# Byte displacements of the TensorE operands inside their SBUF buffers, by place in the turn, stage and chunk

## What is computed

```python
h = x + 0.5 * swiglu(rmsnorm(x), w1g, w1u, w1d)           # FFN 1
B, C, V, Z, Gc, Gp = split(rmsnorm(h) @ w_in)             # one input projection
y_conv = (B * conv3(C * V)) @ w_conv_out                  # 3 taps, causal
y_pool = grouped(trailing means of Z) @ w_pool_group      # windows 2, 4, 8, 16
h = h + (sigmoid(Gc) * y_conv + sigmoid(Gp) * y_pool) @ w_o
h = h + 0.5 * swiglu(rmsnorm(h), w2g, w2u, w2d)           # FFN 2
y = rmsnorm(h)
```

## Time and profile before

| | |
|---|---|
| median of three runs | 2799.03 us |
| the profiled execution, its own time | 2799.0 us |
| its span, first to last instruction | 2797.2 us |
| TensorE, matmuls busy | 2780.8 us, 99% of the span |
| VectorE busy | 1537.5 us, 55% |
| ScalarE busy | 1052.3 us, 38% |
| DMA | 412.27 MB, 147 GB/s |

### The profile page before, as it was taken

The page is one execution under the profiler, slowest core; times in us unless marked ns, Lnnn a source line. Parts: engine busy times, 40 slices in busy tenths (PEclk is TensorE's granted clock), DMA queues, the critical chain, the costliest instruction groups (busy, mean ns, idle before and its releaser), DMA issues.

```text
span 2797.2 us, 47809 instructions
## 1 busy us (share of the span) xinstructions
PE 2780.8 (99%) x18725; PEld 2777.2 (99%) x18725; DVE 1537.5 (55%) x2166; ACT 1052.3 (38%) x1283; POOL 12.3 (0%) x22
## 2 busy tenths in 40 slices
PE   8999999999999999999999999999999999999998
PEld 8999999999999999999999999999999999999998
DVE  6555455554555585555555555575555555555555
ACT  5333333333333453333333334363333333333334
POOL 0000000000000000000000000000000000000000
PEclk9999999999999999999999999999999999999999
DMA  6444444444444444444445444454444444444443
GB/s 196 151 143 142 139 146 142 142 142 142 142 143 143 141 137 151 151 149 141 157 138 158 151 150 142 150 158 151 151 150 150 150 150 150 150 150 150 150 150 105
DMA packets 347876, 412.27 MB, mean 147 GB/s; under 512 B 13039, under 2 KB 283503, under 8 KB 347446
## 3 DMA queue, kind: packets, MB, share of 16 engines
q1 hardware_dynamic: 347264, 410.24, 46.4%
q0 software_dynamic: 560, 1.32, 0.2%
HBM read 408.42 MB, written 3.32 MB: 147 GB/s over the span
## 4 chain that ended last, share of the span: by engine, by line
PE 98%; ACT 1%; DVE 0%; issue 0%; DMA 0%; SPq 0%; ACTq 0%; DVEq 0%
PE bank L408 33%; PE bank L409 33%; PE bank L407 32%; DMA acc<-in_x_sample 0%; ACT tb L710 0%; ACT w_hi L670 0%; PE bank L654 0%; SPq L312 0%; DVE w_lo L925 0%; DVE tok L997 0%; DVE xn_lo L978 0%; ACT h L729 0%; DVE h L1094 0%; PE bank L628 0%; PE bank L474 0%
## 5 line engine op out<-in xcount | busy, mean ns | idle before, releaser
L925 DVE TENSOR_TENSOR w_lo<-raw,w_hi 128x1024 fp32r<-128x1024 f32 x772 | 944.0, 1226 | 1037.7 <-ACT w_hi L670 1036.7
L670 ACT ACTIVATE w_hi<-raw 128x1024 fp32r<-128x1024 f32 x772 | 815.0, 1058 | 1341.6 <-PE bank L409 1340.4
L407 PE MATMUL bank<-xn_hi,w_hi 128*128 128x320 f32 (+2 forms) x4224 | 1314.1, 311 | 2.7 <-DVE xn_lo L978 2.7
L409 PE MATMUL bank<-xn_hi,w_lo 128*128 128x320 f32 (+2 forms) x4224 | 1316.3, 312 | 0.0
L408 PE MATMUL bank<-xn_lo,w_hi 128*128 128x320 f32 (+2 forms) x4224 | 1312.0, 311 | 0.0
L407 PEld LDWEIGHTS bank<-xn_hi,w_hi 128*128 128x128 f32 x4224 | 793.6, 188 | 3.1 <-issue 3.1
L408 PEld LDWEIGHTS bank<-xn_lo,w_hi 128*128 128x128 f32 x4224 | 793.7, 188 | 0.0
L409 PEld LDWEIGHTS bank<-xn_hi,w_lo 128*128 128x128 f32 x4224 | 792.7, 188 | 0.0
L408 PE MATMUL bank<-hid_lo,w_hi 128*128 128x320 f32 (+1 forms) x1952 | 608.2, 312 | 0.0
L409 PE MATMUL bank<-hid_hi,w_lo 128*128 128x320 f32 (+1 forms) x1952 | 606.5, 311 | 0.0
L407 PE MATMUL bank<-hid_hi,w_hi 128*128 128x320 f32 (+1 forms) x1952 | 600.0, 307 | 0.3 <-issue 0.3
(11 more groups left out here) (109 smaller groups left out, 489.1 us busy)
## 6 DMA issues: line engine op xcount, KB each, us to landing
raw<-in_w_ffn_gate SPq DMA_DIRECT2D x176, 512.0 KB, 3.5
raw<-in_w_ffn_up SPq DMA_DIRECT2D x176, 512.0 KB, 3.5
raw<-in_w_ffn_down SPq DMA_DIRECT2D x176, 512.0 KB, 3.6
raw<-in_w_in SPq DMA_DIRECT2D x176, 512.0 KB, 3.5
raw<-in_w_conv_out SPq DMA_DIRECT2D x32, 512.0 KB, 3.8
raw<-in_w_o SPq DMA_DIRECT2D x32, 512.0 KB, 3.7
raw<-in_w_pool_group SPq DMA_DIRECT2D x4, 512.0 KB, 4.0
out<-acc SPq DMA_DIRECT2D x8, 256.0 KB, 3.0
```

The lines of the kernel that those rows point to most:

```text
L407: pe.matmul(out, slot_hi(slot, col, col + P), hi, start=start, stop=False)
L409: return pe.matmul(out, slot_lo(slot, col, col + P), hi, start=False, stop=stop)
L670: act.activation(slot_hi(n % SLOTS), raw[:, n % RAW, :], ACT.Copy).then_inc(hi_done, 1)
L925: dve.tensor_tensor(slot_lo(n % SLOTS), raw[:, n % RAW, :], slot_hi(n % SLOTS).bitcast(F32), ALU.subtract).then_inc(lo_done, 1)
```

## The change

Nothing is added to or taken from the instructions. Only the places of operands inside their buffers change, and a slot becomes 64 floats (256 bytes) longer. Displacements are in floats of four bytes.

```diff
-XH_SHIFT, XL_SHIFT = (0, 0, 0, 0), (16, 8, 32, 48)
-HH_SHIFT, HL_SHIFT = (0, 0, 0, 0), (16, 16, 8, 8)
+XH_SHIFT = ((0, 0, 16, 16), (16, 16, 32, 32), (48, 48, 0, 0))
+XL_SHIFT = ((16, 8, 32, 48), (32, 24, 48, 40), (64, 56, 16, 8))
+HH_SHIFT = ((0, 0, 0, 0), (0, 0, 0, 0), (0, 0, 0, 0), (16, 16, 8, 8), (0, 0, 0, 0))
+HL_SHIFT = ((32, 32, 40, 40), (16, 16, 8, 8), (4, 4, 12, 12), (0, 0, 0, 0), (24, 24, 32, 32))
...
-SLOT = CHUNK
-WH_SHIFT, WL_SHIFT = (0, 0, 0, 0), (0, 0, 0, 0)
+SLOT = CHUNK + 64
...
+W_SPREAD = ((0, 0), (0, 8), (0, 0), (0, 8), (0, 16), (0, 16), (0, 32), (0, 32))
+W_FFN1 = 4 * ((0, 0),) + 4 * ((0, 8),) + 4 * ((0, 16),) + 4 * ((0, 32),) + W_SPREAD
+W_POOL = POOL_CHUNKS * ((0, 0),)
+W_CONV = (4 * ((0, 8),) + 4 * ((0, 16),) + 4 * ((0, 32),) + 4 * ((0, 0),) + 4 * ((0, 24),) + 4 * ((0, 4),)
+          + W_SPREAD)
+W_MIX = 4 * ((0, 8),) + 4 * ((0, 16),) + 4 * ((0, 32),) + 4 * ((0, 0),) + W_SPREAD
+W_FFN2 = 4 * ((0, 8),) + 4 * ((0, 16),) + 4 * ((0, 32),) + 4 * ((0, 24),) + W_SPREAD
+
+def w_place(n):
...
-        def x_hi(k, first):
-            at = k * ROW + XH_SHIFT[k // 4]
-            return xn_hi[:, at + first:at + T]
+        def x_hi(norm, k):
+            at = k * ROW + XH_SHIFT[norm][k // 4]
+            return xn_hi[:, at + first_of(norm):at + T]
...
-        def slot_lo(slot, first=0, last=CHUNK):
-            at = slot * SLOT + WL_SHIFT[slot]
+        def slot_lo(n, first=0, last=CHUNK):
+            at = n % SLOTS * SLOT + w_place(n)[1]
             return w_lo[:, at + first:at + last]
```

More of the change, by code:

```diff
@@ L78, with stage_of @@
 N_ALL = N_FFN2 + FFN_TURNS * FFN_CHUNKS
+W_SPREAD = ((0, 0), (0, 8), (0, 0), (0, 8), (0, 16), (0, 16), (0, 32), (0, 32))
[6 more added lines that the diff above has]
+def w_place(n):
+    if n < N_POOL:
+        return W_FFN1[(n - N_FFN1) % FFN_CHUNKS]
+    if n < N_CONV:
+        return W_POOL[n - N_POOL]
+    if n < N_MIX:
+        return W_CONV[(n - N_CONV) % CONV_CHUNKS]
+    if n < N_FFN2:
+        return W_MIX[(n - N_MIX) % MIX_CHUNKS]
+    return W_FFN2[(n - N_FFN2) % FFN_CHUNKS]
+def stage_of(n):
+    return sum(n >= first for first in (N_POOL, N_CONV, N_MIX, N_FFN2))
 B0, C0, V0, Z0, GC0, GP0 = 0, D, 2 * D, 3 * D, 3 * D + D // 2, 4 * D + D // 2
@@ L195, in build, with x_lo, g_hi, g_lo @@
         bank = [ctx.enter_context(nc.psum_tensor(f"bank{b}", [P, 512], F32)) for b in range(8)]
-        def x_hi(k, first):
-            at = k * ROW + XH_SHIFT[k // 4]
-            return xn_hi[:, at + first:at + T]
[L202 to L207, removed]
+        def x_hi(norm, k):
+            at = k * ROW + XH_SHIFT[norm][k // 4]
+            return xn_hi[:, at + first_of(norm):at + T]
+        def x_lo(norm, k):
+            at = k * ROW + XL_SHIFT[norm][k // 4]
+            return xn_lo[:, at + first_of(norm):at + T]
+        def g_hi(stage, t, width):
+            at = t * ROW + HH_SHIFT[stage][t]
             return hid_hi[:, at:at + width]
-        def g_lo(t, width):
-            at = t * ROW + HL_SHIFT[t]
+        def g_lo(stage, t, width):
+            at = t * ROW + HL_SHIFT[stage][t]
             return hid_lo[:, at:at + width]
-        def slot_hi(slot, first=0, last=CHUNK):
-            at = slot * SLOT + WH_SHIFT[slot]
+        def slot_hi(n, first=0, last=CHUNK):
+            at = n % SLOTS * SLOT + w_place(n)[0]
             return w_hi[:, at + first:at + last]
-        def slot_lo(slot, first=0, last=CHUNK):
-            at = slot * SLOT + WL_SHIFT[slot]
+        def slot_lo(n, first=0, last=CHUNK):
+            at = n % SLOTS * SLOT + w_place(n)[1]
             return w_lo[:, at + first:at + last]
@@ L404, in _, with three_passes, x_of @@
             LOW, HIGH = (0, 1, 2, 3), (4, 5, 6, 7)
[L406 to L409, removed]
+            def three_passes(out, n, col, hi, lo, start, stop):
+                pe.matmul(out, slot_hi(n, col, col + P), hi, start=start, stop=False)
+                pe.matmul(out, slot_hi(n, col, col + P), lo, start=False, stop=False)
+                return pe.matmul(out, slot_lo(n, col, col + P), hi, start=False, stop=stop)
+            def x_of(n, half, k, first_token):
+                norm = (0, 1, 1, 1, 2)[stage_of(n)]
+                return half(norm, k)[:, first_token - first_of(norm):]
             def project(n, banks, first_token, norm=None, between=None):
@@ L696, in stage, with hid_split @@
                     body(n0 + loops * chunks, chunks, last_work)
-            def hid_split(tiles, width, src=None):
+            def hid_split(n, tiles, width, src=None):
                 for t in tiles:
@@ L872, in work @@
                     sigmoids(tb, tb, tiles, LIVE)(n)
-                    hid_split(tiles, LIVE)
+                    hid_split(n, tiles, LIVE)
                 return work
@@ L1085, in work @@
                                               ALU.mult).then_inc(hid_done, 1)
-                        hid_split(tiles, width)
+                        hid_split(n, tiles, width)
                     return work
```

35 lines of the change are left out of this document (18 added, 17 removed).

## The result

The kernel after takes **2812.69 us**, median of 4 runs (2812.18 to 2813.23), beside 2798.99 us (2798.93 to 2799.34) for the kernel before on the same chip. The ratio is 1.0048 (95% interval 1.0036 to 1.006): slower by 13.7 us. I had forecast 2797 and faster. The time lies inside the range given (2770 to 2817), but on the wrong side of no change.

A forecast was written before the change was run, and what follows sets the result against it. The prediction took TensorE's matmul start distances as the bound. Row terms priced at 0.055 us a chunk summed to -2.1 us, with displaced weights at 0, so 2799.0 became 2797 us, range 2770 to 2817.

The forecast's parts named there:

- What bounds it: All three passes: TensorE is busy 2780.8 of 2797.2 us, so time is 18528 matmuls by their start distance.
- The signs that I had named: Profile after: FFN 2 about 5 us shorter, FFN 1 within 1 us, mix 1 to 2 us longer.
- Which bytes count: All operands: only each start in floats modulo 64 (256 bytes) matters; the longer slot costs nothing.
- The terms of the rows: Moving rows: FFN 2 -4.8, FFN 1 c = 2 +2.4, its `hid` -2.4, mix `hid` +1.8, convolution +0.9; sum -2.1 us.
- The bound of one step a chunk: Chunks with displaced low weights: each changes by -0.055 to +0.055 us, thus -34 to +34 us over 616 chunks.
- Two paces: Steady running in the trace: only an upper pace and a lower one, 0.05 to 0.06 us a chunk below.
- The short first pass: `hid` in FFN 2: a pass can cost 10 ns less than its neighbours if the two reads start well apart.
- taken as before: Other convolution and mix pairs, FFN 2 c = 2 and 3, `hid` of pooling, convolution, FFN 2: same or unseen, no change.
- the slower rival: Displaced weights lose the lower pace, in `hid` of the convolution and FFN 2, then projections: +17 us, 2814 us; chance 0.21.
- the zero for displaced low weights: 616 of 772 chunks get a displaced low weight; its effect was taken as 0 by the nearest rows.
- a lower pace can be had in more chunks: Faster rival: displaced weights open the lower pace in 308 chunks, -17 us, 2780 us, chance 0.30; extreme 2748, chance 0.05.
- The last rival, no effect: Whole kernel: two independent SBUF read ports make operand places irrelevant, so 2799 us; chance 0.08.

The follow-up runs named there:

- rows-only kernel: Kernel before with only the moving rows at the places of the kernel after; weights at 0, slot 1024 floats: 2808.12 us, ratio 1.0031.
- steady_a: Kernel before with one displacement set per stage as far as possible, FFN 1 at (0; 32), weights 0, longer slot: 2786.87 us, ratio 0.9956.
- enter_16_8_w8: steady_b with c = 0 of FFN 1's projections at (0; 16) in place of (0; 8), low weights still at 8: 2780.76 us, ratio 0.9927.
- steady_b: steady_a with FFN 1 at (0; 8), its low weights at 8, and low weights 8 for 24 elsewhere: 2769.44 us twice, 2782.97 and 2783.38.
- enter_by_hid: Against the 2771.77 us kernel: FFN 1's projections all at (0; 32), its `hid` tiles 0 and 1 at (0; 8) instead of c = 0: 2772.73 us.

## Why the prediction was wrong

**What bounds it: right.** TensorE's start distances and nothing else, before and after; clock 1.00, no wait for `w_lo`.

**The signs that I had named.** FFN 2 was to be 5 us shorter and is 3.68 longer; FFN 1 was to stand within 1 us and is 6.98 longer. The mix is 1.67 longer, inside the 1 to 2 forecast, and that is in part luck: its `hid` gave 1.2 of the 1.8, its projections, put at nothing, 0.4.

**Which bytes count: right as far as tested.** Three kernels that leave the mutual distances modulo 256 bytes alone stand at 2799.

**The terms of the rows: half right, sum wrong.** Forecast -2.1 us, measured for the rows alone +8.7. The terms taken from pairs that the trace had (FFN 1 c = 2, its `hid`, the mix, FFN 2 c = 0 and 1) have the right sign in the rows-only kernel. They are smaller where a gain was hoped for (-3.1 for -4.8, -1.2 for -2.4), because a change of displacements costs some products on the way and the lower pace isn't always reached: in the rows-only trace c = 0 of FFN 2 takes 3.49 us, its first products 436 to 442 ns and its last three 433, and of the four `hid` chunks of a turn of FFN 1 that went to (0; 32) two reach 3.63. By the table, the terms with a price came to +0.3 us for -2.1, and the groups put at nothing, with the pooling, to 9.1. The prices used a step of 0.055 us; the traces have 0.053.

**The bound of one step a chunk: wrong.** "Two paces" was a reading of single rows. At 322 columns there are at least three, 3.58 and 3.52 in the earlier trace rows and 3.47 in steady_a; at 336 the chunk c = 0 of the kernel after, 3.73 us, is a third one above the old upper pace, eight even products of 467 ns, and c = 2 and 3 of the rows-only kernel take 3.70. The short first pass in the earlier trace rows was misread too: unrounded it is 140 ns beside 146 and 147, not 10 ns less, and it has both of its operands at 0, so it says nothing for reads that start well apart.

**The step that failed first** is the one in which pairs without a row were "taken as before". For `hid` in FFN 2 that was a chunk at the lower pace, the floor of the stage, and a move from a floor has one direction. It cost 5.3 us, and 1.4 in the convolution. I had written exactly that under the slower rival ("the `hid` chunks of FFN 2 can only lose") and put it down to the weights, and left it out of the sum.

**The step that failed second** is the zero for displaced low weights, with the sentence "only the difference of the two places counts". Weights alone cost 10.0 us. All operands count with their mutual distances: c = 1 of FFN 2 takes 3.47 to 3.56 us by the projection. The test that I had named for it (a dependence on the projection) is what the profile shows.

**The assumption under both** was that a pair has a pace. Equal displacements went at two: (0; 32) at 3.62 before and 3.68 in steady_a; (48; 56) with low weights at 24 at 3.47 and 3.52 within one execution of steady_a; 220 unedited chunks changed with 44 edited ones; c = 2 of enter_16_8_w8 by turns. Where the sets change from chunk to chunk, as they do before and after, most of the stream is on its way between paces: from the second turn of FFN 1 on, 196 of 240 chunks of the kernel after have unequal products (140 before, none in steady_b). That would also be why rows and weights don't add.

**The rivals.** The slower one gave 2814, and 2812.69 came. Its place was right as far as it named one: `hid` in the convolution and FFN 2 lost 1.2 + 3.9 = 5.1 us, for 6.6 computed from 120 chunks (by the table of the change only 90 of them get a displaced low weight, 5.0 us). Its 17 us are no more than "half of all displaced chunks", and that 13.7 came so near is in part luck: beyond the 5.1 us there are 8.6, mainly in FFN 1 (7.0), which the rival hadn't singled out; of that, the loss of c = 2 (2.7) was in my own forecast, as 2.4, for the rows. Its mechanism (displaced weights) is one half; rows do it as well. That a lower pace can be had in more chunks was true too, by displacements other than these: in steady_b all chunks of FFN 2 from its second turn on, and all of the convolution but the first three of `hid` in a turn, take 3.47 us. The last rival, no effect, is refuted. The Trainium skill (TensorE: Matmul & The Clock Gate, "Step-by-step: what each phase is for") gives TensorE two independent read ports and says that loading weights does not take read bandwidth from the running matmul. This case does not agree that the place is free: by the places of rows and weights alone the same 18725 instructions take from 2769.4 to 2812.7 us. Whether it is the two reads that meet, no run here shows.

## What to carry to other kernels

Where TensorE is full and its granted clock is 1.00, read the distance over a whole chunk of equal products: if equal shapes go at different paces, where operands start within 256 bytes is worth a try, here 1%. Use one set of displacements for as long a stretch as possible, and look for the floor in a uniform run, not in a table read off mixed ones. And take several executions: a set that is at its floor in one can be at the next step in another, and a stretch at other displacements ahead of it can settle which.

## What the hardware showed that I had not expected

**The time of a product comes in steps.** In steady running three passes took 433 or 440 ns with 320 columns (3.47 and 3.52 us for eight), 453 or 460 with 336. The step is 53 ns in 8 products, 6.7 ns in one, which is 16 cycles of the granted 2.4 GHz. From 320 to 336 columns the lower pace rises by 20 ns, which is the 48 columns more of three passes at 2.4 GHz; by that, the lower paces lie 33 ns above the columns' own time (3 by 320 / 2.4 GHz = 400 ns, 3 by 336 / 2.4 = 420 ns). At 322 columns steady_a's chunks also go at 433 ns a product, so two columns more cost nothing there. Chunks in between, such as 3.70, have unequal products. One such cycle in the kernel after, FFN 1, c = 0 of the fourth projection, the first passes of the second to fifth product:

```profile
509.10 0.32 PE L434 MATMUL bank<-xn_hi,w_hi 128*128 128x336 f32 x1
...
509.57 0.32 PE L434 MATMUL bank<-xn_hi,w_hi 128*128 128x336 f32 x1
...
510.06 0.31 PE L434 MATMUL bank<-xn_hi,w_hi 128*128 128x336 f32 x1
...
510.51 0.32 PE L434 MATMUL bank<-xn_hi,w_hi 128*128 128x336 f32 x1
```

These three products take 0.47, 0.49 and 0.45 us, though their operands have the same places modulo 256 bytes.

**The pace has a memory**: in an even stream it outlasts the chunk, a turn of 24 chunks and the whole of FFN 1 (steady_a at 3.68 us, steady_b at 3.63), and after equal instructions steady_a and enter_by_hid leave the waits at its start at 3.68 and 3.62.

**What stays open** is the mechanism itself. That reads of rows and of weights meet inside 256 bytes is what the dependence on mutual distances suggests; no run separates it from the writes of VectorE and ScalarE, whose places were displaced with the reads. Nor is it known which entries lead to the lower pace: (0; 8) to (0; 32) did, (0; 16) to (0; 8) with low weights at 8 did in two projections of four. Whether the period is shorter than 256 bytes is open too. And the executions of steady_b near 2783 us have no trace; that their 14 us lie in FFN 1 follows from the kernels that differ from it only there and don't have them.
